# A two-layer hybrid token mixer and ConvFFN on one core: the post-norm gain moved into the PSUM eviction, the normalisation boundaries shared by VectorE and GpSimd, and the Ln/Exp table load placed earlier

## The chip, the cores and the metric

One core of a Trainium2 chip runs the whole kernel. The metric is the device time of one execution in microseconds (us); lower is better. The times of a kernel are given as the median of several runs.

## The reference

Two layers (DEPTH 2) work on 256 latent tokens and 256 context tokens of width 1024, in float32. What matters here is how each layer joins its parts:

```python
for l in range(DEPTH):
    need_ctx = l < DEPTH - 1                  # the last layer needs latent tokens only
    h_l = modulate(rms_norm(x, g_pre_mix), mod_l[0], mod_l[1])
    h_c = modulate(rms_norm(ctx, g_pre_mix), mod_c[0], mod_c[1])
    ...
    y_l = merge_branches((gla_l, att_l, lru_l), p_l[11], w_branch[l], w_out[l])
    x = x + mod_l[2] * rms_norm(y_l, g_post_mix)
    ...
    h_l = modulate(rms_norm(x, g_pre_ffn), mod_l[3], mod_l[4])
    x = x + mod_l[5] * rms_norm(conv_ffn(h_l, ...), g_post_ffn)
```

Here `rms_norm(x, g) = x * rsqrt(mean(x*x) + eps) * g` and `modulate(x, shift, scale) = x * (1 + scale) + shift`; the context tokens go the same way with their own modulation. So between the last matmul of one part (`out`, `down`) and the first matmul of the next (`up`, the next layer's `gqk`) there are two norms in a row: the post-norm of the branch, the addition to the stream x, and the pre-norm of the sum.

## The kernel before, in words

The stream x is held transposed in SBUF, as KT = 8 tiles of 128 channels x 512 tokens (columns 0 to 255 context, 256 to 511 latent). In layer 1, after its mixing, only the latent half is worked on (c0 = 256), so the tiles there are 128x256. All weights stream from HBM in 352 units of 512 KB through a ring of seven buffers. Each unit is split into a high and a low part: ScalarE writes `whi` (L399) and VectorE writes the difference `wlo` (L745), both two units ahead of use. TensorE multiplies hi by hi, hi by lo and lo by hi (`part`, L1252), so every activation too must stand as a high and a low half, `hh` and `hl` for the norms' output.

Every engine runs its own program, written out by hand in order, and they meet only at semaphores. `edge(u)` on ScalarE and VectorE evicts the pair of units that has just ended and prepares the unit two ahead.

A norm boundary goes through these steps, each with its line:

1. ScalarE evicts the last pair of `out` or `down`: a Square into `sqm` or `sq` (L451, L454) and a Copy into `mixed` or `y2` (L452, L455; the trace calls the tile y). Then it makes one more `whi`.
2. TensorE sums the squares over channels with a matrix of ones into PSUM bank 6 (`sum_squares`, L1272).
3. ScalarE makes rstd = exp(-0.5 ln(mean + eps)) with an Ln and an Exp (`rstd_made`, L499, L500). These need their own activation table, loaded by `preload_act_table_set` (L528, L724, L731).
4. VectorE's `residual`: for each of the 8 tiles, branch * gain * rstd (L872, an instruction for each 256-column half, since context and latent tokens have different gains), then x + that (L876).
5. ScalarE squares x two tiles at a time as they come (`squares_of_x`, L505), TensorE sums again (L1272), ScalarE makes the second rstd.
6. VectorE's `split_h` and ScalarE's `make_h` by turns, two tiles at a time: VectorE nt = x * gain * rstd (L855), ScalarE hh = nt + shift, rounded to the matmul's format (L513), VectorE hl = nt + shift - hh (L862). TensorE's first unit waits for four tiles of `hl`, its second for all eight (`ready`).

There are five such places: the start of layer 0 (step 6 only counts, for each half after its modulation columns come), `out` to `up` in layer 0 (full width), `down` of layer 0 to `gqk` of layer 1 (full width; here VectorE also makes gains and clears and fills the small tiles `lrh` and `lrl`, L907 to L912), `out` to `up` in layer 1 (half width), and the end (steps 1 to 4, half width), after which one DMA stores the output (L329). GpSimd issues a few DMAs and makes 16 squares l_a*l_a of 128x1024 (L386); at the boundaries it is idle.

## Time and profile before

| what | us |
|---|---|
| median of 3 runs | 2162.42 (2162.36 to 2172.7) |
| the profiled execution | 2166.79 |
| its span | 2165.1 |
| busy: TensorE (PE) / VectorE (DVE) / ScalarE (ACT) / GpSimd (POOL) | 2003.4 / 1123.6 / 940.5 / 49.0 |

The span runs from the first to the last instruction that the profiler saw; 1.7 us of the profiled execution lie around it. The profiled execution is 4.4 us above the median. Busy time is the time in which an engine has an instruction under way; a TensorE that is busy 93% of the span need not be running at its peak, since it spends part of that at half its clock. The chain that ended last lies 81% on TensorE and 11% on VectorE.

### The profile page before, as it was taken

Reading aid. Unit: us, or ns where it says so; the run is one execution under the profiler, and the core shown is the slowest. Engines: PE = TensorE matmul, PEld = TensorE weight load, DVE = VectorE, ACT = ScalarE, POOL = GpSimd, SP = SyncE. Lnnn points to the kernel's source line nnn. Section 1 sums busy time; section 2 is a strip of 40 time slices with the busy share of each in tenths; the row PEclk is TensorE's granted clock in tenths of the full one; section 3 lists DMA queues with packets and bytes.
Section 4 is the critical chain, followed back from the end, with each engine's and each line's share of the span. In section 5 each row is a group of like instructions: output and inputs, shape, how many; then the busy total and the mean of one; then the engine's idle time right before and its main releaser. Section 6 shows DMA issues by size and latency. Waiting matters only on the chain.

```text
span 2165.1 us, 26791 instructions
## 1 busy us (share of the span) xinstructions
PE 2003.4 (93%) x11200; PEld 1641.2 (76%) x11200; DVE 1123.6 (52%) x1591; ACT 940.5 (43%) x1261; POOL 49.0 (2%) x65
## 2 busy tenths in 40 slices
PE   4999989899999999789999998899898999989997
PEld 2877866678777777467777785778777888988997
DVE  2555344644555333355555324654445667757874
ACT  2433144454655322343333323443343777545653
POOL 1000000000000000000000000000000111000000
PEclk8999999999999999999999999999999999999998
DMA  7211111123222445325544432111211444544653
GB/s 277 66 44 57 40 44 49 39 85 95 94 92 89 166 159 180 108 99 182 172 171 165 168 97 78 59 59 49 74 59 49 143 149 141 166 147 139 184 185 107
DMA packets 67513, 245.01 MB, mean 113 GB/s; under 512 B 7600, under 2 KB 8640, under 8 KB 67264
## 3 DMA queue, kind: packets, MB, share of 16 engines
q1 hardware_dynamic: 64544, 233.86, 33.3%
q0 software_dynamic: 1696, 5.24, 0.8%
q10 hardware_dynamic: 1152, 4.19, 0.5%
q8 instruction: 89, 1.46, 0.3%
q14 instruction: 32, 0.26, 0.0%
HBM read 242.21 MB, written 1.05 MB: 112 GB/s over the span
## 4 chain that ended last, share of the span: by engine, by line
PE 81%; DVE 11%; ACT 4%; issue 2%; DMA 1%; SPq 0%; ACTq 0%; DVEq 0%
PE ps L1252 61%; PE ps L1242 4%; PE ps L1526 2%; PE ps L1183 2%; PE ps L1364 2%; DVE wlo L745 2%; PE ps L1436 2%; DMA wraw<-in_weights 1%; ACT whi L399 1%; DVE state L1005 1%; PE ps L1457 1%; PE ps L1272 1%; PE ps L1192 1%; PE ps L1353 1%; DVE x L876 1%
## 5 line engine op out<-in xcount | busy, mean ns | idle before, releaser
L745 DVE TENSOR_TENSOR wlo<-wraw,whi 128x1024 fp32r<-128x1024 f32 x352 | 433.5, 1234 | 563.8 <-ACT whi L399 563.5
L399 ACT ACTIVATE whi<-wraw 128x1024 fp32r<-128x1024 f32 x352 | 370.4, 1055 | 420.0 <-PE ps L1252 272.0
L1252 PE MATMUL ps<-hh,whi 128*128 128x512 f32 (+1 forms) x1760 | 416.5, 359 | 32.9 <-DVE hl L862 23.2
L1252 PE MATMUL ps<-hl,whi 128*128 128x512 f32 (+1 forms) x1760 | 401.3, 351 | 0.0
L1252 PEld LDWEIGHTS ps<-hh,whi 128*128 128x128 f32 x1760 | 293.4, 194 | 108.6 <-issue 64.3
L1252 PE MATMUL ps<-hh,wlo 128*128 128x512 f32 (+1 forms) x1760 | 365.2, 348 | 1.6 <-DVE wlo L745 1.6
L1252 PEld LDWEIGHTS ps<-hl,whi 128*128 128x128 f32 x1760 | 297.8, 194 | 42.8 <-issue 2.2
L1252 PEld LDWEIGHTS ps<-hh,wlo 128*128 128x128 f32 x1760 | 286.4, 191 | 45.1 <-issue 4.9
L773 DVE SCALAR_TENSOR_TENSOR fa<-ps,par,fa 128x510 f32<-128x510 f32 (+1 forms) x176 | 100.1, 610 | 15.0 <-ACT fa L462 13.5
L1252 PE MATMUL ps<-bh,whi 128*128 128x512 f32 (+1 forms) x384 | 86.0, 346 | 3.3 <-ACT whi L399 3.3
L462 ACT ACTIVATE fa<-ps,par 128x512 f32<-128x512 f32 (+1 forms) x88 | 54.0, 664 | 69.9 <-PE ps L1252 69.9
L1252 PE MATMUL ps<-bl,whi 128*128 128x512 f32 (+1 forms) x384 | 83.0, 339 | 0.0
L1252 PE MATMUL ps<-fh,whi 128*128 128x512 f32 (+1 forms) x352 | 78.9, 342 | 0.0
L1252 PE MATMUL ps<-fl,whi 128*128 128x512 f32 (+1 forms) x352 | 76.7, 336 | 0.0
L1252 PEld LDWEIGHTS ps<-bh,whi 128*128 128x128 f32 x384 | 62.8, 191 | 17.0 <-issue 6.2
L1252 PE MATMUL ps<-bh,wlo 128*128 128x512 f32 (+1 forms) x384 | 74.6, 337 | 0.0
L751 DVE COPY ada_rows<-ps 128x512 f32<-128x512 f32 x24 | 16.6, 690 | 104.8 <-PE ps L1183 104.8
L1252 PEld LDWEIGHTS ps<-bl,whi 128*128 128x128 f32 x384 | 63.3, 193 | 7.6
L1252 PE MATMUL ps<-fh,wlo 128*128 128x512 f32 (+1 forms) x352 | 68.8, 336 | 0.0
L1252 PEld LDWEIGHTS ps<-bh,wlo 128*128 128x128 f32 x384 | 61.2, 191 | 7.5
L1252 PEld LDWEIGHTS ps<-fh,whi 128*128 128x128 f32 x352 | 57.5, 190 | 9.7 <-issue 3.1
L1252 PEld LDWEIGHTS ps<-fl,whi 128*128 128x128 f32 x352 | 57.6, 190 | 6.9
(204 smaller groups left out, 2472.5 us busy)
## 6 DMA issues: line engine op xcount, KB each, us to landing
wraw<-in_weights SPq DMA_DIRECT2D x352, 512.0 KB, 3.6
wada<-in_w_ada SPq DMA_DIRECT2D x80, 512.0 KB, 4.2
ada_first<-in_w_ada ACTq DMA_DIRECT2D x8, 512.0 KB, 18.4
ada_first<-in_w_ada SPq DMA_DIRECT2D x8, 512.0 KB, 19.9
wgate<-in_w_gate POOLq DMA_DIRECT2D x16, 256.0 KB, 2.8
x<-in_xt SPq DMA_DIRECT2D x1, 2048.0 KB, 10.1
out_x<-x SPq DMA_DIRECT2D x1, 1024.0 KB, 4.5
par<-in_params POOLq DMA_DIRECT2D x1, 370.0 KB, 9.3
```

Source lines behind the costliest of these rows:

```text
L399: A_(whi[u % HI][:], wraw[RING_W[u] % RAW][:], ACT.Copy).then_inc(s_hi, 1)
L462: ins = A_(fa[j][:, f, c0:], pair_[:, f, c0:], ACT.Identity, scale=pcol(l, "fw")[:, t + 2 * FT:t + 2 * FT + 1], bias=pcol(l, "fb")[:, t:t ...
L745: V.tensor_tensor(wlo[s][:], wraw[s][:], whi[u % HI][:].bitcast(F32), ALU.subtract).then_inc(s_lo, 1)
L773: return V.scalar_tensor_tensor(o[:, :, a], v[:, :, b], pcol(l, name)[:, tile:tile + 1], o[:, :, a], ALU.mult, ALU.add)
L876: V.tensor_tensor(x[:, k, c], x[:, k, c], src[:, k, c], ALU.add).then_inc(s_x, 1)
L1005: ins = V.scalar_tensor_tensor(state[:, d, p + 1], state[:, d, p], g_end[:, d, c:c + 1], kv_, ALU.mult, ALU.add)
L1183: ins = mm(ps[32 * j:32 * j + 32, k if k < 4 else 5, :], csil32[:, 4 * r + j, :], w[:, j % 2, :], start=r == 0, stop=r == 1, tile_position ...
L1242: ins = mm(dst[:, r // 2, 256 * (r % 2):256 * (r % 2 + 1)], x_[:, UK * h + kk, r * P:(r + 1) * P], w[:, kk, :], start=first, stop=h == m - ...
L1252: ins = mm(dst[:, r, c:], w[:, kk, r * P:(r + 1) * P], x_[:, UK * h + kk, c:], start=h == 0 and k in (0, 2) and kk == 0, stop=h == m - 1 a ...
L1364: ins = mm(ps[:, 4 + v, cc], state[:, d, p, v * P:(v + 1) * P], gl_qd[:, d, cc], start=False, stop=d == 1 and p == NCH - 1, skip_group_che ...
L1436: ins = mm(ps[:, 4 + t, 0:(g + 1) * CTX], aq[:, h, r0:r0 + P], ak[:, h // (AQ // AKV), 0:(g + 1) * CTX], start=True, stop=True)
L1526: ins = mm(ps[:, 4 + 2 * d + g], wgate[:, 2 * d + g, :], xc[:, n, :], start=True, stop=True)
```

## The change

The post-norm gain, gmod, is now applied by ScalarE when it evicts `out` and `down`: the Copy becomes one Copy with a per-partition scale for each tile and each half of the tokens (`scaled`). The residual then is branch * rstd and x + that, full-width instructions of two tensors each. Tiles 2, 5 and 7 of each residual and of each split are GpSimd's, the other five VectorE's. For GpSimd's tiles of the split, GpSimd makes x * rstd, ScalarE applies gain and shift in place and copies the rounded value to `hh` (two steps), and GpSimd subtracts. The Ln/Exp table is loaded after the first edge of `out` and of `down` and not after the last. The gains of the post-norms are made earlier. The output is stored by four DMAs of two tiles each.

```diff
+        POOL_X = POOL_H = (2, 5, 7)
...
+        def wait_h(eng, n, k):
+
+            eng.wait_ge(s_h, n * (KT - len(POOL_H)) + k + 1 - by_pool(POOL_H, k))
+            eng.wait_ge(s_hp, n * len(POOL_H) + by_pool(POOL_H, k))
...
-            sp_.wait_ge(s_x, KT * 2 * DEPTH)
-            sp_.dma_start(out, x[:, :, CTX:TOK]).then_inc(s_out, 16)
-            sp_.wait_ge(s_out, 16)
+            for k in range(0, KT, 2):
+                wait_x(sp_, 2 * DEPTH - 1, k + 1)
+                sp_.dma_start(out[:, k:k + 2], x[:, k:k + 2, CTX:TOK]).then_inc(s_out, 16)
+            sp_.wait_ge(s_out, 16 * KT // 2)
...
+            def residual(n, r, src, c0):
+
+                pool.wait_ge(s_rstd, n + 1)
+                for i, k in enumerate(POOL_X):
+                    nc.gpsimd.tensor_tensor(src[:, k, c0:], src[:, k, c0:], rstd[:, c0:], ALU.mult).then_inc(s_ymp, 1)
+                    pool.wait_ge(s_ymp, r * len(POOL_X) + i + 1)
+                    nc.gpsimd.tensor_tensor(x[:, k, c0:], x[:, k, c0:], src[:, k, c0:], ALU.add).then_inc(s_xp, 1)
+
+            def split_h(n, r, c0, src):
...
+                for i, k in enumerate(POOL_H):
+                    pool.wait_ge(s_xp, (r + 1) * len(POOL_X)) if r >= 0 else None
+                    nc.gpsimd.tensor_tensor(src[:, k, c0:], x[:, k, c0:], rstd[:, c0:], ALU.mult).then_inc(s_ntp, 1)
+                for i, k in enumerate(POOL_H):
+                    pool.wait_ge(s_hhi, KT * n + k + 1)
...
+            def scaled(l, norm, i, dst, pair_):
+
+                act.wait_ge(s_gain, 3 * l + norm)
+                for f in range(2):
+                    for s in segs_of(c0_of(l)):
+                        c = slice(s * CTX, (s + 1) * CTX)
+                        ins = A_(dst[:, 2 * i + f, c], pair_[:, f, c], ACT.Copy, scale=gmod[:, norm, 2 * i + f, s:s + 1])
+                return ins
...
-                    A_(mixed[:, 2 * i:2 * i + 2, c0:], pair_[:, :, c0:], ACT.Copy).then_inc(done, 1)
+                    scaled(l, 1, i, mixed, pair_).then_inc(done, 1)
...
+                    if k in POOL_H:
+                        act.wait_ge(s_ntp, len(POOL_H) * n + by_pool(POOL_H, k))
+                        for s in segs:
+                            c = slice(s * CTX, (s + 1) * CTX)
+                            ins = A_(src[:, k, c], src[:, k, c], ACT.Identity, scale=gmod[:, gain, k, s:s + 1],
+                                     bias=MOD[l][:, 8 * shift + k, s:s + 1])
+                        link(ins)
+                        A_(hh[:, k, c0:], src[:, k, c0:], ACT.Copy).then_inc(s_hhi, 1)
+                        continue
...
-                for u in range(first_unit(l, "y"), first_unit(l, "up") + 1):
+                for u in range(first_unit(l, "y"), first_unit(l, "out") + 1):
                     edge(u)
                 act.preload_act_table_set(LN_EXP)
+                for u in range(first_unit(l, "out") + 1, first_unit(l, "up") + 1):
+                    edge(u)
...
+            def residual(n, r, src, c0):
+
+                mine = [k for k in range(KT) if k not in POOL_X]
+                dve.wait_ge(s_rstd, n + 1)
...
+                for i, k in enumerate(mine):
+                    V.tensor_tensor(src[:, k, c0:], src[:, k, c0:], rstd[:, c0:], ALU.mult).then_inc(s_ym, 1)
+                    if i:
+                        add(i - 1)
+                add(len(mine) - 1)
```

The first place: ScalarE's instructions from the last pair of `out` to the first `hh` in layer 0. Before (sqm holds squares, mixed the branch, whi a weight's high part, ps the PSUM banks):

```order
L451 ACTIVATE sqm<-ps 128x1024
L452 ACTIVATE mixed<-ps 128x1024
L399 ACTIVATE whi_77<-wraw_56 128x1024
L724 ACT_TABLE_LOAD
L499 ACTIVATE rstd<-ps,eps 128x512
L500 ACTIVATE rstd<-rstd 128x512
L505 ACTIVATE sqm<-x 128x1024 x4
L499 ACTIVATE rstd<-ps,eps 128x512
L500 ACTIVATE rstd<-rstd 128x512
L513 ACTIVATE hh<-nt,mod 128x256 x16
```

Now:

```order
L505 ACTIVATE sqm<-ps 128x1024
L470 ACTIVATE mixed<-ps,gmod 128x256 x4
L444 ACTIVATE whi_77<-wraw_56 128x1024
L553 ACTIVATE rstd<-ps,eps 128x512
L554 ACTIVATE rstd<-rstd 128x512
L559 ACTIVATE sqm<-x 128x1024 x4
L553 ACTIVATE rstd<-ps,eps 128x512
L554 ACTIVATE rstd<-rstd 128x512
L581 ACTIVATE hh<-nt,mod 128x256 x4
L573 ACTIVATE nt<-nt,mod,gmod 128x256 x2
L576 ACTIVATE hh<-nt 128x512
```

The table load has left this stretch, one Copy has become four, and tile 2 of the split has two steps where the others have one.

The second place: VectorE at the same boundary, from the first tile of the residual to the split. Before:

```order
L872 SCALAR_TENSOR_TENSOR mixed<-mixed,gmod,rstd 128x256 x2
L876 TENSOR_TENSOR x<-x,mixed 128x512
L872 SCALAR_TENSOR_TENSOR mixed<-mixed,gmod,rstd 128x256 x2
L876 TENSOR_TENSOR x<-x,mixed 128x512
L855 SCALAR_TENSOR_TENSOR nt<-x,gmod,rstd 128x256 x4
L862 SCALAR_TENSOR_TENSOR hl<-nt,mod,hh 128x256 x4
```

These are the last two tiles of eight, and the first of the split's four turns. Now, whole:

```order
L958 TENSOR_TENSOR mixed<-mixed,rstd 128x512 x2
L955 TENSOR_TENSOR x<-x,mixed 128x512
L958 TENSOR_TENSOR mixed<-mixed,rstd 128x512
L955 TENSOR_TENSOR x<-x,mixed 128x512
L958 TENSOR_TENSOR mixed<-mixed,rstd 128x512
L955 TENSOR_TENSOR x<-x,mixed 128x512
L958 TENSOR_TENSOR mixed<-mixed,rstd 128x512
L955 TENSOR_TENSOR x<-x,mixed 128x512 x2
L940 SCALAR_TENSOR_TENSOR nt<-x,gmod,rstd 128x256 x4
L928 SCALAR_TENSOR_TENSOR hl<-nt,mod,hh 128x256 x4
L940 SCALAR_TENSOR_TENSOR nt<-x,gmod,rstd 128x256 x4
L928 SCALAR_TENSOR_TENSOR hl<-nt,mod,hh 128x256 x4
```

VectorE's residual shrinks from 24 instructions to 10; x of tile 1 is its fifth instruction, x of tile 3 its seventh.

The third place: GpSimd at the same boundary, where it had nothing:

```order
L392 TENSOR_TENSOR mixed<-mixed,rstd 128x512 [waits rstd_made]
L394 TENSOR_TENSOR x<-x,mixed 128x512 [waits branch_scaled_by_pool]
L392 TENSOR_TENSOR mixed<-mixed,rstd 128x512
L394 TENSOR_TENSOR x<-x,mixed 128x512 [waits branch_scaled_by_pool]
L392 TENSOR_TENSOR mixed<-mixed,rstd 128x512
L394 TENSOR_TENSOR x<-x,mixed 128x512 [waits branch_scaled_by_pool]
L401 TENSOR_TENSOR nt<-x,rstd 128x512 [waits x_updated_by_pool,rstd_made]
L401 TENSOR_TENSOR nt<-x,rstd 128x512 [waits x_updated_by_pool] x2
L404 TENSOR_TENSOR hl<-nt,hh 128x512 [waits h_hi_made] x3
```

It has six instructions in the residual, then three products and three differences for the split.

## Rows read from the trace of the kernel before

**Rows 1.** Waits of TensorE: who was waited for, total us, times, longest.

```profile
PE ps L1252 <- DVE hl L862: 23.2, 3, 9.7
PE ps L1272 <- ACT sq L505: 22.7, 3, 16.0
PE ps L1272 <- ACT sqm L505: 13.3, 4, 6.9
```

**Rows 2.** Timeline, out to up, layer 0: start, us, engine, instruction, [idle before].

```profile
897.11 1.02 ACT L452 ACTIVATE mixed<-ps 128x1024 f32<-128x1024 f32 x1
898.02 1.06 ACT L399 ACTIVATE whi<-wraw 128x1024 fp32r<-128x1024 f32 x1
...
899.09 1.28 ACT L724 ACT_TABLE_LOAD   x1
...
901.77 0.88 DVE L872 SCALAR_TENSOR_TENSOR mixed<-mixed,gmod,rstd 128x256 f32<-128x256 f32 x2 [1.36 <-ACT rstd L500]
902.68 0.69 DVE L876 TENSOR_TENSOR x<-x,mixed 128x512 f32<-128x512 f32 x1
903.29 0.87 DVE L872 SCALAR_TENSOR_TENSOR mixed<-mixed,gmod,rstd 128x256 f32<-128x256 f32 x2
...
906.12 7.99 PE L1272 MATMUL ps<-sqm,ones 128*128 128x512 f32 x12 [6.87 <-ACT sqm L505]
...
915.13 1.98 PE L1272 MATMUL ps<-sqm,ones 128*128 128x512 f32 x4 [1.02 <-ACT sqm L505]
...
917.15 0.69 ACT L499 ACTIVATE rstd<-ps,eps 128x512 f32<-128x512 f32 x1 [2.07 <-PE ps L1272]
...
918.53 1.67 DVE L855 SCALAR_TENSOR_TENSOR nt<-x,gmod,rstd 128x256 f32<-128x256 f32 x4 [4.54 <-ACT rstd L500]
919.45 1.71 ACT L513 ACTIVATE hh<-nt,mod 128x256 fp32r<-128x256 f32 x4 [0.95 <-DVE nt L855]
...
925.66 2.04 PE L1252 MATMUL ps<-hh,whi 128*128 128x512 f32 x4 [8.55 <-DVE hl L862]
```

**Rows 3.** Timeline, down of layer 0 to gqk of layer 1, ScalarE and VectorE.

```profile
1337.09 0.69 ACT L499 ACTIVATE rstd<-ps,eps 128x512 f32<-128x512 f32 x1 [0.21 <-PE ps L1272]
...
1354.59 0.63 ACT L500 ACTIVATE rstd<-rstd 128x512 f32<-128x512 f32 x1
...
1356.38 1.67 DVE L855 SCALAR_TENSOR_TENSOR nt<-x,gmod,rstd 128x256 f32<-128x256 f32 x4
```

**Rows 4.** Timeline, out to up, layer 1 (half width).

```profile
1941.51 0.47 ACT L499 ACTIVATE rstd<-ps,eps 128x256 f32<-128x256 f32 x1
...
1942.47 0.48 DVE L872 SCALAR_TENSOR_TENSOR mixed<-mixed,gmod,rstd 128x256 f32<-128x256 f32 x1 [1.01 <-ACT rstd L500]
...
1951.29 0.47 ACT L499 ACTIVATE rstd<-ps,eps 128x256 f32<-128x256 f32 x1 [1.22 <-PE ps L1272]
...
1956.19 1.19 PE L1252 MATMUL ps<-hh,whi 128*128 128x256 f32 x4 [4.94 <-DVE hl L862]
```

**Rows 5.** GpSimd's products, one source line: ns min/median/max, first and last start.

```profile
L386 POOL TENSOR_TENSOR l_tr<-l_a x16: 1889/1890/1896, 469.2 to 1835.9; 128x1024 f32<-128x1024 f32 x16
```

**Rows 6.** Timeline around one of those (GpSimd, VectorE).

```profile
1695.69 1.89 POOL L386 TENSOR_TENSOR l_tr<-l_a 128x1024 f32<-128x1024 f32 x1 [6.10 <-ACT l_th L704]
...
1696.60 2.07 DVE L745 TENSOR_TENSOR wlo<-wraw,whi 128x1024 fp32r<-128x1024 f32 x1 [1.36 <-ACT whi L399]
```

**Rows 7.** The weight split on VectorE: ns min/median/max, first and last start.

```profile
L745 DVE TENSOR_TENSOR wlo<-wraw,whi x352: 1212/1226/2074, 33.2 to 2144.4; 128x1024 fp32r<-128x1024 f32 x176
```

**Rows 8.** Windows, layer 0 boundary: length, busy of PE, PEld, DVE, ACT, POOL, then PEclk.

```profile
907.00:909.00 2.00, 2.00 (x4) 0.68 (x2) 1.93 (x5) 1.04 (x1) 0.00 (x0) 0.50 0.00 0
```

**Rows 9.** The end: timeline, and the output's DMA (KB each, us to landing).

```profile
2153.21 0.48 DVE L872 SCALAR_TENSOR_TENSOR y<-y,gmod,rstd 128x256 f32<-128x256 f32 x1 [7.59 <-ACT rstd L500]
...
2160.18 0.63 SPq L329 DMA_DIRECT2D out_x<-x  x1
out_x<-x SPq DMA_DIRECT2D x1, 1024.0 KB, 4.5
```

More of the change, by code:

```diff
@@ L308, in att_items, with by_pool, wait_x @@
             return (0 if l == 0 else 16), [(h, g) for h in range(AQ) for g in range(2 - ng, 2)]
+        POOL_X = POOL_H = (2, 5, 7)
+        def by_pool(tiles_, k):
+            return sum(t <= k for t in tiles_)
+        def wait_x(eng, r, k):
+            d, p = r * (KT - len(POOL_X)) + k + 1 - by_pool(POOL_X, k), r * len(POOL_X) + by_pool(POOL_X, k)
+            eng.wait_ge(s_x, d)
+            eng.wait_ge(s_xp, p) if p else None
+        def wait_h(eng, n, k):
+            eng.wait_ge(s_h, n * (KT - len(POOL_H)) + k + 1 - by_pool(POOL_H, k))
+            eng.wait_ge(s_hp, n * len(POOL_H) + by_pool(POOL_H, k))
         @block.sync
@@ L374, in _ @@
                 pool.dma_start(lrw[:], w_lr[l]).then_inc(s_lrw, 16)
+                if l:
+                    residual(4 * l - 1, 2 * l - 1, y2, c0_of(l - 1))
+                split_h(2 * l, 2 * l - 1, 0, nt0)
                 pool.wait_ge(s_on, HEADS * (l + 1))
@@ L386, in _ @@
                     nc.gpsimd.tensor_tensor(l_tr[:], l_a[:], l_a[:], ALU.mult).then_inc(s_la2, 1)
+                residual(4 * l + 1, 2 * l, mixed, c0_of(l))
+                split_h(2 * l + 1, 2 * l, c0_of(l), nt)
+            residual(4 * DEPTH - 1, 2 * DEPTH - 1, y2, c0_of(DEPTH - 1))
         @block.scalar
@@ L451, in evac_first @@
                     A_(sqm[:, 2 * i:2 * i + 2, c0:], pair_[:, :, c0:], ACT.Square).then_inc(s_sq, 1)
-                    A_(mixed[:, 2 * i:2 * i + 2, c0:], pair_[:, :, c0:], ACT.Copy).then_inc(done, 1)
+                    scaled(l, 1, i, mixed, pair_).then_inc(done, 1)
                 elif name == "down":
                     A_(sq[:, 2 * i:2 * i + 2, c0:], pair_[:, :, c0:], ACT.Square).then_inc(s_sq, 1)
-                    A_(y2[:, 2 * i:2 * i + 2, c0:], pair_[:, :, c0:], ACT.Copy).then_inc(done, 1)
+                    scaled(l, 3, i, y2, pair_).then_inc(done, 1)
                 elif name == "up":
@@ L866, in residual, with low @@
-            def residual(n, src, gain, segs):
-                dve.wait_ge(s_rstd, n + 1)
-                for k in range(KT):
+                def low(k):
+                    if k in POOL_H:
+                        return
+                    dve.wait_ge(s_hhi, KT * n + k + 1)
                     for s in segs:
                         c = slice(s * CTX, (s + 1) * CTX)
-                        ins = V.scalar_tensor_tensor(src[:, k, c], src[:, k, c], gmod[:, gain, k, s:s + 1], rstd[:, c],
-                                                     ALU.mult, ALU.mult)
-                    link(ins)
-                    c = slice(segs[0] * CTX, TOK)
-                    V.tensor_tensor(x[:, k, c], x[:, k, c], src[:, k, c], ALU.add).then_inc(s_x, 1)
+                        ins = V.scalar_tensor_tensor(hl[:, k, c], src[:, k, c], MOD[l][:, 8 * shift + k, s:s + 1],
+                                                     hh[:, k, c].bitcast(F32), ALU.add, ALU.subtract)
+                    ins.then_inc(s_h, 1)
@@ new lines, in split_h @@
+                for k in range(k0, k1):
+                    if k in POOL_H:
+                        if k > k0:
+                            low(k - 1)
+                        continue
+                    wait_x(dve, 2 * l - 1 if shift == 0 else 2 * l, k) if (l or shift) else None
+                    for s in segs:
+                        c = slice(s * CTX, (s + 1) * CTX)
+                        ins = V.scalar_tensor_tensor(src[:, k, c], x[:, k, c], gmod[:, gain, k, s:s + 1], rstd[:, c],
+                                                     ALU.mult, ALU.mult)
+                    ins.then_inc(s_nt, 1)
+                    if k > k0:
+                        low(k - 1)
@@ L898, in _ @@
                     edge(u0)
-                    residual(4 * l - 1, y2, 3, segs_of(c0_of(l - 1)))
+                    residual(4 * l - 1, 2 * l - 1, y2, c0_of(l - 1))
                     dve.wait_ge(s_ada, ADA_CHUNKS)
@@ L1157, in _ @@
                     edge(u)
+                    if l == 0 and u == first_unit(0, "g2", 2):
+                        dve.wait_ge(s_ada, 6)
+                        gains(0, 1)
+                        dve.sem_inc(s_gain, 1)
                     if l == 0 and u == first_unit(0, "out", 2):
                         dve.wait_ge(s_ada, 10)
-                        gains(0, 1)
                         gains(0, 2)
-                residual(4 * l + 1, mixed, 1, segs)
+                        dve.sem_inc(s_gain, 1)
+                residual(4 * l + 1, 2 * l, mixed, c0)
                 dve.wait_ge(s_rstd, 4 * l + 3)
@@ L1166, in _ @@
                     edge(u)
-                    if l == 0 and u == first_unit(0, "down", 1):
+                    if l == 0 and u == first_unit(0, "up", 4):
                         dve.wait_ge(s_ada, 12)
                         gains(0, 3)
-            residual(4 * DEPTH - 1, y2, 3, segs_of(c0_of(DEPTH - 1)))
+                        dve.sem_inc(s_gain, 1)
+            residual(4 * DEPTH - 1, 2 * DEPTH - 1, y2, c0_of(DEPTH - 1))
         @block.tensor
```

60 lines of the change are left out of this document (31 added, 29 removed).

## The prediction

> **What bounds the kernel now.** I read the page first: TensorE is busy 93% of the span and carries 81% of the chain that ended last, so only what TensorE waits for can move the time by much. The list of its waits [rows 1] says where it waits: 23.2 us in three waits for `hl`, and 22.7 and 13.3 us for squares (a few of them those of the branch, not of x). That is nearly all at the norm boundaries that the change touches, about 59 us or 2.7%, and the most that it could win. Then I read the timeline of each boundary. In the full-width one of layer 0 [rows 2] the reader is to see a relay: table load, Ln and Exp, from 901.77 VectorE's residual, TensorE's sums from 906.12, Ln at 917.15, split from 918.53, first matmul of `up` at 925.66. The second full-width one differs in that the table load is not ahead of the Ln: that waits for TensorE's sums [rows 3]. The half-width one is the same relay, shorter [rows 4], and the end has the residual and a DMA [rows 9]. Last I looked at what GpSimd's arithmetic costs [rows 5], and what it does to VectorE beside it [rows 6].
>
> **The rows that decide.** GpSimd's product of 128x1024 takes 1.89 us [rows 5]. Where VectorE starts a weight split (median 1.23 us, [rows 7]) while one runs, the split takes up to 2.07 us [rows 6, 7]. In the row, GpSimd runs from 1695.69 to 1697.58; VectorE starts at 1696.60 and ends at 1698.67, 1.09 us after GpSimd. There are six such meetings (three of 2.07, three of 1.59, which began later under GpSimd's), each over within 1.1 us after GpSimd's end, and none without the stretch: an instruction of VectorE that reads two SBUF tensors stands still until GpSimd's is over, and then needs its whole time less 0.06 us of start. Every VectorE instruction of the residual and of the split reads two SBUF tensors, and so does every GpSimd one. So I add their times where the change would overlap them. The trace has no GpSimd instruction that comes second, so it doesn't show whether VectorE holds GpSimd too; I take it that it does. The Trainium skill, "SBUF — State Buffer", section "Who interferes with whom", states just that: the shared port pair is an exclusive lock, and whichever starts first keeps it for the whole instruction. By that rule the sum stays as below; by its contrary the third rival holds.
>
> **GpSimd's price.** No row has 128x512. It lies between 0.95 (half of 1.89) and 1.89 (nothing depends on size). VectorE's tensor-tensor goes from 1.23 [rows 7] to 0.69 [rows 2], so 0.15 is fixed; the same for GpSimd gives 1.0 at 512 and 0.56 at 256, near the lower end. I take these. The Trainium skill, "GPSIMD Engine Reference", section "3.1 Elementwise — side-by-side cycle accounting", measures 4497 ns for an add of 2048 columns, an estimated 1.15 us for 512; this trace's 1.89 for 1024 is cheaper than that slope. By that price the sum is the first rival's.
>
> **The change, part by part.**
>
> 1. *Eviction and table.* `scaled` issues instructions with a per-partition operand, 256 wide. Their nearest row has four in 1.71 us, a spacing of 0.41 [rows 2]; four take 1.65 where the Copy took 0.91 to the next start (897.11 to 898.02): +0.74; two half-width ones 0.83 for some 0.47: +0.35. In layer 0's `out` the load of 1.28 us leaves: Ln would come at 897.11 + 1.65 + 1.07 = 899.83 instead of 900.37 (load's end): -0.55. In layer 1's `out`: 1.28 less 0.35, -0.95. At `down` the load was hidden already and Ln waited only 0.21 us [rows 3]: 0.74 - 0.21 = +0.55. At the end ScalarE waits longer for TensorE than 0.35: 0. The other pairs' scaled evictions and the load's new place lie beside some 20 us of matmuls: 0. Bounds at a place: between +0 (the Copy's own rate) and +1.1 (no overlap, 0.5 each).
>
> 2. *Residual, full width (twice).* Before, a tile took 1.52 us (901.77 to 903.29), eight 12.2. Now VectorE has 10 instructions at 0.61 (902.68 to 903.29) and GpSimd six at 1.0, in line: 6.1 + 6.0 - 0.6 for starts = 11.5. So the last x comes 0.7 earlier. But the first square needs x of tiles 0 and 1. That was at 3.0 us; now tile 1 is VectorE's fifth instruction with four of GpSimd's between, 5 x 0.55 + 4 x 1.0 = 6.7. Tile 3 is the seventh, at 9.7. The squares and sums come bunched: TensorE had 11.0 us from its first sum to the Ln (906.12 to 917.15). After an idle stretch of 6.87 its granted clock is 0.50, which is 1.2 GHz [rows 8]; the last four matmuls, at full clock, took 1.98, so 0.50 each, and the first twelve 7.99 [rows 2], which makes about six of them 0.85 each and the rest 0.50. Now the first sum starts at 7.7 and takes four times 0.85 = 3.4 to 11.1; the other twelve follow back to back, four at 0.85 and eight at 0.50 us: 18.5 from the start, against 15.4. If the clock comes back with the first of them it is 17.1. I take +2.5.
>
> 3. *Split, full width (twice).* Before, from 918.53 to the first matmul at 925.66: 7.1 us, 16 instructions at 0.41. Now the first unit needs `hl` of tiles 0, 1 and 3 from VectorE, behind 14 instructions (tile 4's product stands ahead): 5.7. In the same stretch GpSimd has its three products and tile 2's difference: 4.0. In line 9.7, less 0.1: +2.5. ScalarE's two steps for tile 2 hide behind this. The second unit's `hl` come later too, but hide behind the first unit's 7 to 8 us on TensorE. In layer 1's start VectorE reaches the split 1.2 us after rstd (1355.22 to 1356.38, [rows 3]) because it fills small tiles; GpSimd's first product runs there: -1.0.
>
> 4. *Half width (once).* Residual: VectorE's 10 at 0.35 and GpSimd's 6 at 0.56. The first sum at 4.2, and the Ln, before at 8.8 us (1942.47 to 1951.29, [rows 4]), at about 10.0: +1.2. Split 7 x 0.40 + 4 x 0.56 = 5.0 against 3.95 (Exp ends 0.92 after that Ln began, the first matmul is at 1956.19): +1.1.
>
> 5. *The end.* Residual 6.9 us before (2153.21 to just before 2160.18); now 3.5 + 3.4 - 0.4 = 6.5: -0.5. The store of 1024 KB took 4.5 us to land [rows 9]; the last of four pieces moves a quarter, behind two others that have hardly started: between 0 and -3.0, I take -1.5.
>
> 6. *The start.* GpSimd's products are done long before; VectorE has 12 instructions where it had 16 before TensorE's adaLN sums can go on: between -1.4 and +0.5 (a GpSimd difference in between, ScalarE's second step), I take -0.3.
>
> 7. *Queues.* GpSimd's DMAs for the decay weights now stand behind the split of layer 0's `up`; the weights are wanted some 440 us later: 0. Gains made earlier: 0. No other engine waits behind the new waits.
>
> Sum: layer 0 `up` -0.55 + 5.0; layer 1 start +0.55 + 5.0 - 1.0; layer 1 `up` -0.95 + 2.3; end -2.0; start -0.3 = **+8.0 us**. The profiled execution of 2166.8 would become 2174.8. Against the median, 2162.4 + 8.0, **2170.4 us**.
>
> **Rivals.**
>
> - *GpSimd's instruction is dearer, slower than before.* Here multiply and add read two tensors, L386 one tensor twice. Ten GpSimd instructions stand in line at a full boundary, ten short ones at the half-width one, six at the end. Each 0.1 us more at 512 (half at 256) adds 1.0 + 1.0 + 0.5 + 0.3 = 2.8 us. From 1.1 us on the loss passes 0.5%. At 1.2 us: 8.0 + 5.6 = +13.6, **2176.0**. For it: no row of two different tensors. [...]
> - *No hold between the engines: faster.* Then the residual ends after 6.2 and the split's first part after 6.2. The sums of squares bound instead: first at 4.2, all by 14.3 instead of 15.4. Each full boundary gains 1.9, the half-width one 1.9, the residual at the end 3.3, the store 1.5, the start 0.6, and part 1 gives -0.95: -12.1 in all, **2150.3**. Against it: six stretched splits of six [rows 6].
> - *Only VectorE is held*, while GpSimd may start under it. Then a GpSimd instruction hides up to one of VectorE's: I give back 3.5 at each full boundary, 1.7 and 0.6 at the others: -1.3, **2161.1**.
> - *That the load isn't moved* I leave out: the order has it ahead of `out` and `down` and nowhere else new.
>
> **How the numbers follow.** A measurement here can tell 0.5%, 10.8 us, from no change. The forecast, 0.52, of which 0.07 lies above +10.8 (a dearer handover between the engines); GpSimd dearer 0.28; only VectorE held 0.10; no hold 0.10, of which 0.07 beyond -10.8. So faster 0.07, same 0.58, slower 0.35. The range leaves out the no-hold case and the top of the dear one: 2156 to 2179.
>
> **What would show it.** Right: at the three inner boundaries VectorE's 128x512 products last about 1.5 us and not 0.69 in the residual, x of tile 1 some 6.7 us after rstd, TensorE's waits for `hl` and for squares together longer by 5 us at each full boundary, the Ln right behind `whi` at both `out`s, and the last output piece landing in less than 4.5 us. Wrong: VectorE's durations as before beside GpSimd's (no hold), or GpSimd's 128x512 at 1.2 or more (first rival), or TensorE's clock staying up across the residual, which would take 2 us from each full boundary.

## The result and the profile after

| | before | after |
|---|---|---|
| median of 11 runs each, us | 2165.98 | 2176.76 |
| lowest to highest, us | 2162.36 to 2172.7 | 2174.57 to 2179.89 |
| profiled execution, its span, us | 2166.79, 2165.1 | 2174.57, 2172.8 |
| granted TensorE clock, mean | 0.975 | 0.972 |
| GpSimd busy, us | 49.0 | 107.5 |

The ratio is 1.0048, with a 95% interval of 1.0039 to 1.0057: slower by 0.48%. The profiled executions differ by 7.8 us and the medians by 10.8 us; the profiled one of after happens to be its lowest, so I read places from the profiles and the size of the whole from the medians.

TensorE's waits, the same list as [rows 1] (line waited at, releaser: us in total, times, longest):

```profile
PE ps L1342 <- DVE hl L928: 30.0, 3, 12.2
PE ps L1362 <- ACT sq L559: 26.2, 2, 16.0
PE ps L1362 <- ACT sqm L559: 17.1, 2, 10.2
```

All three groups have grown: `hl` by 6.8 us over three boundaries, and the longest wait for squares of `out` from 6.9 to 10.2 us. The 16.0 us in the second group is the same in both kernels: it is TensorE's wait for the first squares of all, at the start of the kernel, and nothing in the change can shorten it. The timeline of the layer 0 boundary, to be laid beside [rows 2] (start, us, engine, instruction, [idle before]):

```profile
897.97 0.71 ACT L553 ACTIVATE rstd<-ps,eps 128x512 f32<-128x512 f32 x1
...
899.37 2.36 DVE L958 TENSOR_TENSOR mixed<-mixed,rstd 128x512 f32<-128x512 f32 x2
899.42 1.77 POOL L392 TENSOR_TENSOR mixed<-mixed,rstd 128x512 f32<-128x512 f32 x1 [220.72 <-ACT rstd L554]
901.26 1.59 POOL L394 TENSOR_TENSOR x<-x,mixed 128x512 f32<-128x512 f32 x1
901.66 1.75 DVE L955 TENSOR_TENSOR x<-x,mixed 128x512 f32<-128x512 f32 x1
902.82 1.71 POOL L392 TENSOR_TENSOR mixed<-mixed,rstd 128x512 f32<-128x512 f32 x1
903.33 1.74 DVE L958 TENSOR_TENSOR mixed<-mixed,rstd 128x512 f32<-128x512 f32 x1
904.60 1.59 POOL L394 TENSOR_TENSOR x<-x,mixed 128x512 f32<-128x512 f32 x1
904.99 1.75 DVE L955 TENSOR_TENSOR x<-x,mixed 128x512 f32<-128x512 f32 x1
...
907.98 9.38 PE L1362 MATMUL ps<-sqm,ones 128*128 128x512 f32 x16 [10.24 <-ACT sqm L559]
...
910.01 0.68 DVE L958 TENSOR_TENSOR mixed<-mixed,rstd 128x512 f32<-128x512 f32 x1
...
917.39 0.69 ACT L553 ACTIVATE rstd<-ps,eps 128x512 f32<-128x512 f32 x1 [4.07 <-PE ps L1362]
...
918.77 4.80 DVE L940 SCALAR_TENSOR_TENSOR nt<-x,gmod,rstd 128x256 f32<-128x256 f32 x4 [6.88 <-ACT rstd L554]
918.82 4.07 POOL L401 TENSOR_TENSOR nt<-x,rstd 128x512 f32<-128x512 f32 x3 [9.28 <-ACT rstd L554]
...
929.07 2.05 PE L1342 MATMUL ps<-hh,whi 128*128 128x512 f32 x4 [11.71 <-DVE hl L928]
930.68 1.28 POOL L404 TENSOR_TENSOR hl<-nt,hh 128x512 fp32r<-128x512 f32 x1 [2.95 <-ACT hh L576]
```

The reader is to see three things. While both engines have work, VectorE's 128x512 instruction is on record with 1.75 us, and with 0.68 at 910.01, when GpSimd is done. GpSimd's are stretched too (1.59 to 1.77, against 1.28 at 930.68, where it is alone for nearly all of it). And from 901.66 to 904.99 each of the two finishes two instructions: VectorE's starts come every 1.67 us, and so do GpSimd's on average. In the split, four of VectorE's 128x256 instructions that took 1.67 us in [rows 2] take 4.80 us beside three products of GpSimd.

By place, from the last Square of the branch to the next part's first matmul, in us:

| place | before | after | difference | forecast |
|---|---|---|---|---|
| `out` to `up`, layer 0 | 29.47 | 34.39 | +4.92 | +4.45 |
| start of layer 1 | 29.56 | 34.16 | +4.60 | +4.55 |
| `out` to `up`, layer 1 | 18.02 | 20.30 | +2.28 | +1.35 |
| last Square to the end | 14.66 | 12.31 | -2.35 | -2.0 |
| the rest of the span | | | -1.75 | -0.3 |

The places of layer 0 start at these two rows, the first of before and the second of after, and end at the row of the first matmul (925.66 in [rows 2], 929.07 above):

```profile
896.19 1.02 ACT L451 ACTIVATE sqm<-ps 128x1024 f32<-128x1024 f32 x1 [2.64 <-PE ps L1252]
894.68 1.02 ACT L505 ACTIVATE sqm<-ps 128x1024 f32<-128x1024 f32 x1 [2.60 <-PE ps L1342]
```

The four places sum to +9.45 us. The rest of the span, -1.75, is almost all in stretches whose work the change leaves alone. It comes to 2073.4 us before, 2071.6 after, and between 2067 and 2075 in the experiments below, so 2 us of it say nothing about a kernel.

### The profile page after: what moved, and what is told of

Same layout as the page of the kernel before. It is cut to its first block, busy times and chain, and to the rows that moved or that the text cites. A ratio compares the mean times of both kernels' runs of the same rounds, so it can differ in the third digit from the quotient of the medians.

```text
span 2172.8 us, 26845 instructions
## 1 busy us (share of the span) xinstructions
PE 2001.4 (92%) x11200; PEld 1640.9 (76%) x11200; DVE 1118.9 (51%) x1509; ACT 954.6 (44%) x1305; POOL 107.5 (5%) x113
## 4 chain that ended last, share of the span: by engine, by line
PE 81%; DVE 10%; ACT 4%; issue 3%; DMA 1%; SPq 0%; POOL 0%; DVEq 0%; ACTq 0%
PE ps L1342 60%; PE ps L1332 4%; PE ps L1616 2%; PE ps L1273 2%; DVE wlo L816 2%; PE ps L1362 2%; PE ps L1454 2%; PE ps L1526 2%; DMA wraw<-in_weights 1%; ACT whi L444 1%; DVE state L1090 1%; PE ps L1547 1%; PE ps L1282 1%; PE ps L1443 1%; DVE nt L940 1%
```

## Experiments

**1. GpSimd out of the boundaries.** All of the change but GpSimd's share; all eight tiles on VectorE in the new order.

```diff
-        POOL_X = POOL_H = (2, 5, 7)
+        POOL_X, POOL_H = (), ()
```

> Theory (GpSimd costs the boundaries their time, because it and VectorE hold each other; the other parts of the change gain a little): 2159.5 us, about 6.5 below the kernel before and 17 below the changed kernel. By place against before: out to up of layer 0 -1.3, start of layer 1 -0.2, out to up of layer 1 -1.95, end -3.4. Rival A (what costs is the rest: all squares of x late because VectorE takes product and sum alternately, the new order of the split, the four scaled copies in place of one): about 2172 us, as much as the changed kernel less the 1 or 2 us that GpSimd's share is worth. VectorE's instructions of 128x512 should last 0.68 us in the boundaries by both.

Measured: median 2160.25 us, ratio to before 0.9966 (0.9953 to 0.9979). The four places take 28.33, 27.90, 16.36 and 10.9 us, which is 1.14, 1.66, 1.66 and 3.8 less than before; at the start of layer 1 I had expected only 0.2 less. So what costs the change its time is GpSimd's share: 16.5 us by the medians (of two comparisons), 17.7 by the four places. The rest of the change gains 6.3. Rival A is out.

**2 and 3. One share at a time.** `POOL_X, POOL_H = (2, 5, 7), ()` shares the residual only, `(), (2, 5, 7)` the split only.

> Theory: sharing the residual alone costs 2.6 us (layer 0, whole norm), 2.0 us (start of layer 1), 2.2 us (half norm) and 1.1 us (end) over the kernel with no GpSimd part: 8 us over it, 2167.5 us, about +1.5 over the kernel before. VectorE's products of 128x512 last 1.7 us beside GpSimd's in the residual, 0.68 us in the split. Rival A: within 1 us of the kernel with no GpSimd part.

> Theory: sharing the split alone costs 3.2 us, 2.4 us and 1.2 us at the three boundaries and 0.3 us at the start: 7 us over the kernel with no GpSimd part, 2166.5 us, within 1 us of the kernel before; with the share of the residual the two costs add up to the changed kernel's 17 us over the one with no GpSimd part, less 2 us where one part covers the other. Rival B (the shares only cost together, since the residual delays the split's start): under 3 us over the kernel with no GpSimd part.

Measured: residual shared 2169.96 us, ratio 1.0019 (1.0010 to 1.0028); split shared 2163.04 us, 0.9985 (0.9974 to 0.9995). Over experiment 1, by place in the profiles: the residual's share costs 3.48, 3.82 and 3.95 us at the three boundaries and 1.5 us at the end (1.16 of it in the residual itself); the split's costs 2.54, 2.67 and 1.77. At the two full boundaries both together cost 6.06 and 6.26 us, which is the sum of the two (6.02 and 6.49), so neither covers the other. At the half norm both cost 3.94, less than the sum 5.7: there the sixteen sums of squares of x take from 5.22 to 6.54 us in these profiles, by how soon TensorE's clock comes back, and that noise is as large as the term. I had expected too little of the first and 7 us of the second. The 2.8 us that the medians give the second lies in rival B's range. But B's mechanism, that the split costs only behind a delayed residual, is out: the split alone costs 2.54 and 2.67 us at the full boundaries. In size it is open: the medians of experiments 1 and 3 differ by only 2.8 us, though their profiled spans differ by 5.5 and the three boundaries by 7.0. Experiment 1's profile was 3.8 us longer than experiment 3's between the first matmul of layer 1 and the end of its `out`, where the code is the same, and experiment 3's profiled execution lies 2.4 us above its median; both are of the size of the gap. Whether the 7 us of the places or the 2.8 of the medians is the share's lasting price isn't settled.

**4. GpSimd fills in place of products.** The same places, waits and signals, but GpSimd writes zeros and reads no tile (one of its four lines shown; the fill in the sum's place goes to the branch's tile too, not to x).

```diff
-nc.gpsimd.tensor_tensor(src[:, k, c0:], src[:, k, c0:], rstd[:, c0:], ALU.mult).then_inc(s_ymp, 1)
+nc.gpsimd.memset(src[:, k, c0:], 0.0).then_inc(s_ymp, 1)
```

> Every product, sum and difference of GpSimd in the boundaries is replaced by a fill of the same tile with zeros: GpSimd has the same places, waits and signals, but reads no tile of SBUF, and the normed stream of its three tiles is left out of the output. Theory (the hold is between instructions that read two tiles each): VectorE's instructions of 128x512 last 0.68 us beside the fills, and x is complete about 6.5 us after the residual's start against 12.5; out to up of layer 0 takes 25 us or less, the whole kernel 2152 us or less. Rival C (any work of GpSimd in SBUF slows VectorE, through the port's use or the semaphores): VectorE's instructions beside the fills last over 0.9 us. Rival D (nothing is held, GpSimd is merely slow): VectorE is at 0.68 us here as it must be, and so it should have been in the changed kernel, where it was at 1.74.

Measured: 2150.41 us in two executions, ratio 0.9923 (0.9903 to 0.9943); `out` to `up` of layer 0 takes 25.51 us, just over the 25 expected. The timeline of the residual in layer 0's `out`:

```profile
899.84 0.52 POOL L392 MEMSET mixed<- 128x512 f32 x1 [220.70 <-ACT rstd L554]
900.42 0.52 POOL L394 MEMSET mixed<- 128x512 f32 x1
900.89 0.52 POOL L392 MEMSET mixed<- 128x512 f32 x1
901.03 0.68 DVE L955 TENSOR_TENSOR x<-x,mixed 128x512 f32<-128x512 f32 x1
901.47 0.52 POOL L394 MEMSET mixed<- 128x512 f32 x1
901.63 0.68 DVE L958 TENSOR_TENSOR mixed<-mixed,rstd 128x512 f32<-128x512 f32 x1
```

VectorE runs at 0.68 us with GpSimd writing beside it; x is complete 6.1 us after the residual's start (12.5 in the changed kernel), and the first square comes at 3.13. Writes of as many bytes under the same semaphores hold nothing, so rivals C and D are out. The kernel is 16.2 us under before in its comparison. Two engines that shared the real work without a hold would gain less than that, since a fill lasts 0.52 us and a product alone 1.28. That the no-hold rival's number was 2150.3 us is chance: it stands 12.1 us under a before of 2162.4.

**5. GpSimd copies in place of products.** One tile read, one written, to see if the hold needs two reads.

```diff
-nc.gpsimd.tensor_tensor(src[:, k, c0:], src[:, k, c0:], rstd[:, c0:], ALU.mult).then_inc(s_ymp, 1)
+nc.gpsimd.tensor_copy(src[:, k, c0:], rstd[:, c0:]).then_inc(s_ymp, 1)
```

> In the changed kernel each of GpSimd's products, sums and differences is replaced by a copy of one tile into the same place: one tile read, one written; the output leaves out the norm and the residual of three tiles. Theory (the hold is between instructions that read two tiles): VectorE's 128x512 instructions stay at 0.68 us beside them and the residual ends 6.1 to 8 us after it starts, as it did beside the fills. Rival F (any read of SBUF by GpSimd holds VectorE): 1.0 to 1.7 us each beside the copies, and the residual ends 9 us or more after it starts.

Measured: 2155.71 us, one execution. The same stretch, and at the end a copy (with the rounding to the matmul's format) that has no VectorE instruction beside it:

```profile
900.11 1.07 POOL L392 COPY mixed<-rstd 128x512 f32<-128x512 f32 x1
900.63 1.09 DVE L958 TENSOR_TENSOR mixed<-mixed,rstd 128x512 f32<-128x512 f32 x1
901.24 0.95 POOL L394 COPY x<-mixed 128x512 f32<-128x512 f32 x1
901.65 1.09 DVE L955 TENSOR_TENSOR x<-x,mixed 128x512 f32<-128x512 f32 x1
...
904.69 0.68 DVE L958 TENSOR_TENSOR mixed<-mixed,rstd 128x512 f32<-128x512 f32 x1
...
923.76 0.62 POOL L404 CAST hl<-nt 128x512 fp32r<-128x512 f32 x1 [2.93 <-ACT hh L576]
```

My theory that only two-tile reads hold fell: VectorE's instruction takes 1.09 us beside a copy. One of each takes 1.02 us together, that is VectorE's 0.60 and 0.42 more. A product or sum of GpSimd costs 1.07 more, a fill nothing. The 0.95 to 1.07 us on record for a copy beside VectorE are stretched by the hold; alone it takes 0.62. So a copy adds 0.20 us less than it takes alone. A product does nearly the same: 1.28 us alone, 1.07 added, 0.21 less. At 128x256 it is 0.73 alone and 0.52 added for a product (experiment 1 against the changed kernel), 0.40 and 0.20 for a copy. In all four forms the two engines work one after the other, but for 0.2 us. x was complete at 8.58 us, between the ranges of the theory and of rival F, so the durations decide, and they are rival F's.

**6. One tile instead of three.** `POOL_X, POOL_H = (7,), ()`: GpSimd takes one tile of each residual.

> GpSimd takes tile 7 of each residual and nothing of the split; all else as in the kernel with no GpSimd part. Theory (while both have work, one instruction of each takes 1.67 us together, that is 0.55 and 1.12 us one after the other): fourteen instructions of VectorE at 0.6 us and two of GpSimd at 1.07 us more give x complete 10.6 us after the residual's start at a full norm, against 9.7 us with none and 12.5 us with three tiles; the first square 5.3 us after it against 3.1 us. Rival H (the engines work beside each other and three tiles were only too many): x complete 8.6 us after the start.

Measured: x complete 10.65 us after the residual's start, the first square at 5.26 us; 2167.94 us, ratio 0.9999 (0.9986 to 1.0013). Both numbers come out as the sum of both engines' times gives them, so rival H is out. By these prices no distribution of tiles shortens the residual while VectorE has work, since every instruction moved to GpSimd costs the pair 1.07 us and saves 0.60; that is worked out, and other distributions were not run. Over experiment 1, one tile costs 1.11, 2.50, 1.39 and 0.65 us at the four places, 5.7 in all, where three cost 12.7 (3.48, 3.82, 3.95 and 1.50); the profiled spans say 4.7 and 9.5. So one tile costs nearly half of what three do and not a third, because its two instructions stand right at the start, ahead of the first square, which they make 2.13 us later where three tiles make it 4.27. The medians say 7.7 of 9.7, but they come from different comparisons, and one tile's interval alone is some 3 us to either side. Between 901.72 and 905.67 VectorE does three instructions in 3.95 us (three times 0.60 and twice 1.07 make 3.94), and later ones every 0.60:

```profile
901.72 2.36 DVE L957 TENSOR_TENSOR mixed<-mixed,rstd 128x512 f32<-128x512 f32 x2
904.00 1.74 DVE L954 TENSOR_TENSOR x<-x,mixed 128x512 f32<-128x512 f32 x1
905.67 0.68 DVE L957 TENSOR_TENSOR mixed<-mixed,rstd 128x512 f32<-128x512 f32 x1
```

**7. Tables and store as before,** on the kernel of experiment 1.

```diff
-            for k in range(0, KT, 2):
-                wait_x(sp_, 2 * DEPTH - 1, k + 1)
-                sp_.dma_start(out[:, k:k + 2], x[:, k:k + 2, CTX:TOK]).then_inc(s_out, 16)
-            sp_.wait_ge(s_out, 16 * KT // 2)
+            wait_x(sp_, 2 * DEPTH - 1, KT - 1)
+            sp_.dma_start(out, x[:, :, CTX:TOK]).then_inc(s_out, 16)
+            sp_.wait_ge(s_out, 16)
...
-                for u in range(first_unit(l, "y"), first_unit(l, "out") + 1):
+                for u in range(first_unit(l, "y"), first_unit(l, "up") + 1):
                     edge(u)
                 act.preload_act_table_set(LN_EXP)
-                for u in range(first_unit(l, "out") + 1, first_unit(l, "up") + 1):
-                    edge(u)
```

(and the same for `down`)

> On the kernel with no GpSimd part, with the activation tables loaded where the kernel before loads them and x stored by one transfer after its last tile. Theory (each of these two parts of the change gains what lies on the path): +1.4 us from the last Square to the residual of out of layer 0, +1.05 us at out of layer 1 (half tiles), nothing at down, since the kernel before has that load finished ahead of the last Square, and +2.0 to 2.3 us between the last sum and the end: 4.5 us over the kernel with no GpSimd part, 2164.7 us. Rival E (the load is hidden beside the sums of squares on TensorE, and the store's fixed part dominates): under 1.5 us in all.

Measured: 2166.86 us, ratio 0.9997 (0.9988 to 1.0007); 6.6 us over experiment 1 by the medians, 4.8 by the profiled spans. By place: Square to residual 6.11 against 4.71 (+1.40) at layer 0's `out`, 4.54 against 3.45 (+1.09) at layer 1's, 4.69 against 4.70 at `down`; from the last x to the end 4.99 against 2.64 (+2.35). ScalarE there:

```profile
898.45 1.08 ACT L441 ACTIVATE whi<-wraw 128x1024 fp32r<-128x1024 f32 x1
899.55 1.28 ACT L788 ACT_TABLE_LOAD   x1
900.84 0.69 ACT L550 ACTIVATE rstd<-ps,eps 128x512 f32<-128x512 f32 x1
```

These two parts of the change gain 4.8 us by the places, which is most of what experiment 1 gained over before. Rival E is out.

**8. The split's old order,** on the kernel of experiment 1, twice.

```diff
-                for k in range(k0, k1):
...
-                    ins.then_inc(s_nt, 1)
-                    if k > k0:
-                        low(k - 1)
-                low(k1 - 1)
+                for k in range(k0, k1, 2):
+                    for kk in (k, k + 1):
...
+                        ins.then_inc(s_nt, 1)
+                    low(k)
+                    low(k + 1)
```

> On the kernel with no GpSimd part, the split written in the order of the kernel before (two scaled tiles, then their two low parts). Theory: the order of the change (scaled 0, 1, low 0, scaled 2, low 1) puts a scaled tile ahead of the first unit's last low part; going back gains 0.6 us at out to up of layer 0, 0.2 us at the half norm, nothing at the start of layer 1 (where what is waited for is elsewhere): 0.8 us less, 2159.4 us, at the edge of what the runs tell, so the places in the profile decide. Rival: none of it, the order is free.

> The kernel of the run with the old order and no GpSimd part again, beside the next one: 2157 us. Theory (the order gains at each boundary what the split's rows showed, 0.51, 0.51 and 0.13 us): the three Ln-to-first-matmul times repeat within 0.1 us (8.57, 9.21, 4.96).

Measured: 2157.23 us, ratio 0.9956 (0.9942 to 0.9970), and 2156.39 us, 0.9943 (0.9930 to 0.9955). Ln to first matmul is 8.57, 9.21 and 4.96 us, and 8.57, 9.21 and 4.97 again, against 9.08, 9.72 and 5.09 in experiment 1: 0.51, 0.51 and 0.13 us. I had expected nothing at the start of layer 1, and it is there too. The medians fell by 3 to 4 us, more than these 1.2; the intervals overlap with experiment 1's, and the rest is not explained by the places.

**9 and 10. TensorE kept busy,** on the kernel of experiment 8: matmuls of constants into PSUM bank 7, which nothing reads.

```diff
+            def fill(n):
+                for _ in range(n):
+                    mm(ps[:, 7, :], ones[:], scanmask[:].rearrange("p n c -> p (n c)"), start=True, stop=True)
...
+                fill(5 if l == 0 else 3)
                 pe.wait_ge(s_rstd, 4 * l + 2)
                 for j in range(4):
                     sum_squares(4 * l + 2, j, sqm, c0)
+                fill(8 if l == 0 else 4)
```

(and 5 and 8 at the start of layer 1; experiment 9 had twice these numbers)

> On the kernel with no GpSimd part, the split in the old order, and matmuls of constants into the unused bank 7 while TensorE waits at the boundaries (10 and 16 of 128x512 at the full norms, 6 and 8 at the half norm). Theory: TensorE comes out of its 6 and 9 us waits at 1.2 GHz (0.86 us for a sum that takes 0.43 us later, 2.04 us for four matmuls that take 1.07 us), and kept busy it stays at 2.4 GHz: second Ln of layer 0 at 12.9 us after the residual's start against 14.54, the first matmuls of up in pairs of 0.27 us, 1 us more gained behind each of the three boundaries: 6 us under the kernel with no GpSimd part with the order's 0.8 us, 2154 us. Rival G (the chip lowers the clock elsewhere for the added work, or the fillers run at 1.2 GHz and end late): 2160 us or more, with granted clocks below 0.97 in the stretches between.

> As the run with fillers, with half as many (5 and 8 at the full norms, 3 and 4 at the half norm), since one filler took 0.87 us, being two passes, and not the 0.43 us that they were counted by. Theory: they end 1 us or more ahead of what TensorE then waits for, so nothing is late, and the clock stays up: first sum of squares in 0.43 us each, second Ln of layer 0 at 12.9 us after the residual's start, 13 at the start of layer 1 and 7.3 at the half norm, first four matmuls of a part in 1.1 us in place of 2.0: 5 to 7 us under the kernel with the old order alone, 2151 us. Rival G (the work is taken back by a lower clock elsewhere): granted clock between the boundaries below that of the kernel with the old order, and 2156 us or more.

Measured: with twice the fillers 2163.64 us, ratio 0.9988 (0.9979 to 0.9997), which is slower than without. I had counted a filler at 0.43 us, and it is two passes, 0.87 us: the sixteen ended 4.6 us late, and `up` began 13.1 us after the Ln in place of 8.6. The number lies in rival G's range by that part of it, fillers that end late, but they ran at 2.4 GHz and the mean granted clock was 0.984. With half of them 2153.58 us, ratio 0.9931 (0.9917 to 0.9944), the fastest kernel here that leaves nothing out: 13.5 us under before in the same comparison. TensorE at layer 0, where the rows x10 and x16 are five and eight fillers of two passes each:

```profile
901.34 4.45 PE L1362 MATMUL ps<-scanmask,ones 128*128 128x512 f32 x10
907.48 1.96 PE L1356 MATMUL ps<-sqm,ones 128*128 128x512 f32 x4 [1.68 <-ACT sqm L557]
909.79 1.99 PE L1356 MATMUL ps<-sqm,ones 128*128 128x512 f32 x4 [0.36 <-ACT sqm L557]
912.20 3.79 PE L1356 MATMUL ps<-sqm,ones 128*128 128x512 f32 x8 [0.43 <-ACT sqm L557]
915.83 7.03 PE L1362 MATMUL ps<-scanmask,ones 128*128 128x512 f32 x16
924.60 1.17 PE L1336 MATMUL ps<-hh,whi 128*128 128x512 f32 x4 [1.74 <-DVE hl L926]
```

TensorE now waits for each pair of squares, where it had been behind them, and `up`'s first four matmuls take 1.17 us against 2.04 without the fillers. The windows of experiment 1 and of this kernel (length, busy of PE, PEld, DVE, ACT, POOL, then PEclk) show the two levels, 1.2 and 2.4 GHz; first experiment 1,

```profile
908.00:910.00 2.00, 2.00 (x4) 0.96 (x3) 2.00 (x4) 1.06 (x1) 0.00 (x0) 0.50 0.00 0
924.70:926.70 2.00, 2.00 (x5) 1.61 (x6) 2.00 (x6) 0.91 (x2) 0.00 (x0) 0.50 0.00 0
```

then with the fillers:

```profile
908.00:910.00 2.00, 1.64 (x5) 0.57 (x4) 2.00 (x5) 1.06 (x1) 0.00 (x0) 1.00 0.00 0
924.70:926.70 2.00, 2.00 (x9) 1.66 (x10) 1.81 (x6) 1.42 (x4) 0.00 (x0) 1.00 0.00 0
```

The second Ln comes 12.89 us after the residual's start at both full norms, as forecast, against 14.18 and 13.53. At the start of layer 1 only 0.29 of the 0.64 us reach the first matmul, since the small tiles that VectorE fills there are then what the split waits for. At the half norm the Ln comes at 8.39 us and not at 7.3 (8.58 without fillers). TensorE's three fillers there run at 2.4 GHz (granted clock 1.00 from 1931.6 to 1934.3), it waits 1.66 us, and then the granted clock falls while it is busy with the sums (0.79 in the window from 1936.1 to 1938.1, then 0.50):

```profile
1936.01 5.78 PE L1356 MATMUL ps<-sqm,ones 128*128 128x256 f32 x16 [1.66 <-ACT sqm L557]
1938.00:1940.00 2.00, 2.00 (x7) 1.55 (x6) 0.89 (x3) 1.18 (x2) 0.00 (x0) 0.50 0.04 8
```

The whole gained 2.8 us by the medians and 4.7 by the profiled spans, where I had said 5 to 7, and the two intervals overlap. The places show 1.30, 0.29 and 0.20 us at the three boundaries, and that is what can be called shown, with the 0.9 us of `up`'s first four matmuls. Rival G isn't what took the rest: the mean granted clock rose from 0.974 to 0.984.

## Why the prediction was right, by its steps

The forecast was +8.0 us in the profile and 2170.4 for the median. The profile gave +7.8. The median of the comparison, 2176.76, stands against a before of 2165.98 there, and the forecast started from 2162.4; the ratio is the better measure, 1.0048 against a forecast of 1.0037. That the profile gave +7.8 is partly luck: its four places gave +9.45 where the steps below said +8.35, and -1.75 came from stretches that the change leaves alone. The mechanism and the sign were right; the size was low by 1 to 3 us.

- **The mechanism.** VectorE and GpSimd hold each other when both read SBUF. That VectorE also holds GpSimd was assumed; the pitch of 1.67 us on both engines, the fills (experiment 4) and the single tile (6) show it. The Trainium skill, "SBUF — State Buffer", section "Who interferes with whom", says that a VectorE instruction with two SBUF inputs contends with a GpSimd instruction that reads SBUF, and not with one that only writes it. The fills (VectorE at 0.68 us) and the products (pitch 1.67 us) agree with it. It also calls the hold an exclusive lock. The copies agree with that once their length alone is taken (0.62 us, 0.42 added), and so does the trace of before: GpSimd's products of 128x1024 took 1889 to 1896 ns [rows 5], through all six meetings, and VectorE's instruction ended 1.08 to 1.09 us after them whether it had begun some 1.0 us before their end or 0.5. Had the two shared a bandwidth, GpSimd's would have been stretched too. One small reading of mine was off: 1.09 us is VectorE's 1.23 less 0.14, and not less 0.06.
- **The bound.** I put the most that the change could win at 59 us. 16.0 of them are the wait at the start of the kernel, so it was 43; no term of the sum used it.
- **Step 1, eviction and table.** Forecast -0.55, +0.55, -0.95; measured -0.89, +0.22, -0.85 from Square to residual, the last with the residual at 4.30 before and 3.45 after. Four scaled copies of 256 columns take 1.42 us to the next start (0.91 before), so +0.51 and not the +0.74 taken from the row of `hh`. Experiment 7 gives the load alone: 1.40 and 1.09 us.
- **Step 2, residual.** Forecast +2.5 from residual to Ln at each full norm; measured +2.64 and +1.95. The parts were off in ways that cancel: the first sum came at 8.6 us and not at 7.7, and the last x at 12.5 and not 11.5, but the sixteen sums took 9.38 and 8.71 us where I had 10.8 with the clock down. The size is given by GpSimd's instruction: 1.07 us in alternation.
- **Step 3, split.** Forecast +2.5; measured +3.17 and +2.43. Of the first, 2.6 us is GpSimd's share (9.08 to 11.68) and 0.5 the new order (experiment 8), which I had not priced. At the start of layer 1 the credit of 1.0 us failed: it assumed that GpSimd's first product runs while VectorE has other work, but that work reads SBUF too and is held:

```profile
1359.81 4.07 POOL L401 TENSOR_TENSOR nt<-x,rstd 128x512 f32<-128x512 f32 x3 [8.61 <-ACT rstd L554]
1360.08 1.28 DVE L998 TENSOR_TENSOR lrl<-lrw,lrh 128x256 fp32r<-128x256 f32 x1 [1.51 <-ACT lrh L610]
1361.28 3.67 DVE L940 SCALAR_TENSOR_TENSOR nt<-x,gmod,rstd 128x256 f32<-128x256 f32 x4
```

  The place still came out at +4.60 against +4.55, because steps 1 and 2 fell 0.3 and 0.55 us short of their forecasts there: that is luck.

- **Step 4, half width.** Forecast +1.2 and +1.1; measured +1.94 and +1.19. The first is low by 0.7 us, and neither GpSimd's price nor the clock explains it: the pitch of the pair is 0.86 us, VectorE's 0.34 and 0.52 more where I had 0.56, and from the first sum to the Ln it took 5.56 us where I had 5.8. The first sum came at 5.2 us and not at 4.2. VectorE, still busy with a weight split, started 0.29 us behind GpSimd here, so that five of GpSimd's instructions and not four stood in line with the five up to x of tile 1, and the square took 0.8 us to the first sum where my 4.2 leaves some 0.5:

```profile
1947.83 0.95 POOL L392 TENSOR_TENSOR mixed<-mixed,rstd 128x256 f32<-128x256 f32 x1 [106.11 <-ACT rstd L554]
1948.12 1.81 DVE L958 TENSOR_TENSOR mixed<-mixed,rstd 128x256 f32<-128x256 f32 x2
...
1949.85 0.94 DVE L955 TENSOR_TENSOR x<-x,mixed 128x256 f32<-128x256 f32 x1
```

- **Step 5, end.** Forecast -0.5 and -1.5; measured -0.32 and -2.03. Without GpSimd the residual is 5.45 us and the store gives 2.35. The four pieces land in a median of 2.3 us, against the 4.5 of [rows 9]:

```profile
out_x<-x SPq DMA_DIRECT2D x4, 256.0 KB, 2.3
```

- **Step 6, start.** Forecast -0.3; the first matmul on `hh` of layer 0 comes at 54.99 us after and 55.12 before, -0.13.
- **GpSimd's price,** the term that all the others rest on. Forecast 1.0 us at 128x512; measured 1.28 us alone and 1.07 in alternation. I had named 1.2 or more as a sign of the first rival, and by the record that sign came; what counts in the sum is the 1.07. For that rival speaks also that two different tiles are dearer than one read twice: 0.73 us at 256 columns and 1.28 at 512 make an estimated 2.4 at 1024, where L386 takes 1.89. The first rival (dearer) is therefore half true: its slope of 2.8 us for 0.1 us puts 1.07 at +10.0 us, which is near the medians' +10.8, but with the errors above that agreement is partly luck. The price that I estimated from the Trainium skill, "GPSIMD Engine Reference", section "3.1 Elementwise — side-by-side cycle accounting", 1.15 us (a plain quarter of its 4497 ns is 1.12), lies between the two measured numbers. The rival with only VectorE held would have given 2161.1, and is excluded by the pitch.

## What to carry to other kernels

Before work is moved from VectorE to GpSimd, look in the trace for one meeting of the two: where VectorE's instruction ends only after GpSimd's, by nearly its own whole length, the shared work costs the sum of both, and a tile at the head of the relay costs more than its share (one tile 5.7 us by the places, three 12.7). Parts of a change should be priced apart: here the earlier table load and the store in pieces gained 4.8 us, the new order of the split lost 1.2, and the sharing, which cost 16.5, hid both. Where TensorE waits 6 to 9 us in a relay, look at the granted clock after the wait; filler matmuls must be costed by a row of the same type, and end before what is waited for.
